# First transformer block of a three-layer f32 kernel: the projections, the long convolution, the norms and the output product in another order

## What is computed

```python
h = rms_norm(x, pre_mix_g[l])
u = h @ w_in[l]                                   # 256x1024 @ 1024x2560
u_conf, u_sc, u_att, u_lru = jnp.split(u, splits, axis=-1)
y_a = conformer_conv_mixer(...)   # val * sigmoid(gate), causal conv of 31 taps, group norm, silu
y_b = short_conv_mixer(...)       # b_gate * conv of 3 taps (c_gate * xs)
y_c = moba_attention(u_att)       # 256 rows, 4 heads of 64: here plain causal attention with ALiBi
y_d = rglru_mixer(...)            # conv of 4 taps, two gates, a linear scan over the rows, * gelu(gate)
y = jnp.concatenate([y_a, y_b, y_c, y_d], axis=-1) @ w_out[l]
x = x + rms_norm(y, post_mix_g[l])
h = rms_norm(x, pre_mlp_g[l])
m = jnp.square(jax.nn.relu(h @ mlp_w1[l])) @ mlp_w2[l]
x = x + rms_norm(m, post_mlp_g[l])
```

## Time and profile before

| | us |
|---|---|
| median of 3 runs | 1889.55 (1889.2 to 1892.25) |
| the profiled execution: time | 1888.89 |
| the profiled execution: span, first to last instruction | 1887.2 |
| the mixer's block in it | 0.3 to 158.4 |

### The profile page before, as it was taken

How to read it: one execution, slowest core, us unless ns; L and a number is a source line. 1 busy time by engine, 2 the same in 40 slices (tenths; PEclk the granted TensorE clock), 3 DMA queues, 4 the chain that set the end, 5 groups by cost and what they waited for, 6 DMA issues and landing times.

```text
span 1887.2 us, 21638 instructions
## 1 busy us (share of the span) xinstructions
PE 1387.0 (73%) x7036; PEld 562.5 (30%) x7036; DVE 1168.3 (62%) x2679; ACT 597.3 (32%) x1522; POOL 551.6 (29%) x629
## 2 busy tenths in 40 slices
PE   6978999997886555668877875497687855655665
PEld 5835566664331110123222221132232311101010
DVE  2553144125786777685688536866886478677764
ACT  2041111122433333343334323342443243332332
POOL 2002043002433333332333323322333233333432
PEclk9978999998997666779867897799888977776667
DMA  9036478634999999999999999999999999999997
GB/s 336 31 129 241 164 276 335 266 124 185 418 419 420 420 421 421 421 410 418 418 409 396 415 417 420 417 377 417 420 403 415 418 421 413 421 421 421 422 421 292
DMA packets 117966, 680.74 MB, mean 361 GB/s; under 512 B 11694, under 2 KB 13872, under 8 KB 49888
## 3 DMA queue, kind: packets, MB, share of 16 engines
q0 software_dynamic: 78336, 553.68, 71.1%
q1 hardware_dynamic: 39520, 125.71, 17.4%
HBM read 678.30 MB, written 1.05 MB: 360 GB/s over the span
## 4 chain that ended last, share of the span: by engine, by line
DMA 36%; PE 32%; DVE 11%; ACT 4%; issue 3%; DVEq 2%; POOL 2%; ACTq 1%; POOLq 0%
DMA big<-in_peer_uv,expert 33%; PE ps L584 7%; PE ps L742 6%; PE ps L1774 6%; PE ps L1785 6%; DVE big L597 5%; DMA big<-in_w_kv 2%; DVEq L463 2%; POOL big L555 2%; PE ps L328 2%; DMA normed<-in_peer_uv,expert 1%; PE ps L569 1%; ACT placed L632 1%; ACT placed L628 1%; PE ps L746 1%
## 5 line engine op out<-in xcount | busy, mean ns | idle before, releaser
L584 PE MATMUL ps<-big,placed 128*32 128x512 f32 x1992 | 597.5, 797 | 387.3 <-ACT placed L632 385.4
L597 DVE CUSTOM_DVE_ANT_0 big<-big,ps 128x1024 f32<-128x1024 f32 x498 | 595.1, 1219 | 324.1 <-DMA big<-in_peer_uv,expert 307.4
L555 POOL DMA_INDIRECT big<-in_peer_uv,expert x498 | 475.6, 955 | 1028.5 <-PE ps L584 855.1
L628 ACT ACTIVATE placed<-sel,dots 128x32 f32<-128x32 f32 x512 | 163.3, 319 | 776.5 <-DVE dots L597 769.7
L584 PEld LDWEIGHTS ps<-big,placed 128*32 128x32 f32 x1992 | 81.2, 122 | 820.1 <-ACT placed L632 740.1
L742 PE MATMUL ps<-big 128*128 128x512 f32 x384 | 191.7, 636 | 12.7 <-DVE big L1065 6.5
L632 ACT ACTIVATE placed<-placed,gate 128x32 f32<-128x32 f32 x512 | 164.6, 321 | 36.5 <-issue 1.7
L1774 PE MATMUL ps<-ua,big 128*128 128x256 f32 x512 | 116.8, 382 | 0.0
L1785 PE MATMUL ps<-big,sc 128*128 128x512 f32 x256 | 115.5, 595 | 0.0
L742 PEld LDWEIGHTS ps<-big 128*128 128x128 f32 x384 | 71.2, 200 | 129.6 <-issue 108.9
L1774 PEld LDWEIGHTS ps<-ua,big 128*128 128x128 f32 x512 | 98.1, 192 | 26.9 <-issue 15.0
(11 more groups left out here) (349 smaller groups left out, 1318.3 us busy)
## 6 DMA issues: line engine op xcount, KB each, us to landing
big<-in_mlp_w SPq DMA_DIRECT2D x16, 2048.0 KB, 10.9
big<-in_peer_wq SPq DMA_DIRECT2D x2, 8192.0 KB, 26.5
big<-in_w_kv SPq DMA_DIRECT2D x32, 512.0 KB, 15.8
big<-in_peer_wq SPq DMA_DIRECT2D x32, 512.0 KB, 14.1
big<-in_w_in SPq DMA_DIRECT2D x5, 2048.0 KB, 17.6
big<-in_peer_uv,expert POOLq DMA_INDIRECT x530, 14.9
big<-in_w_q SPq DMA_DIRECT2D x16, 512.0 KB, 10.7
big<-in_w_o SPq DMA_DIRECT2D x16, 512.0 KB, 12.8
```

The lines of the kernel that those rows point to most:

```text
L555: nc.gpsimd.indirect_dma_start(out=pair_row(n), out_offset=None, in_=rows, in_offset=bass.IndirectOffsetOnAxis(ap=expert[:, n // TOPK % DE ...
L584: last = nc.tensor.matmul(acc[r:r + TOK, :], placed[:, n % RING, :], pair_row(n)[:, D + BANK * half:D + BANK * (half + 1)], start=(opens a ...
L597: nc.vector.tensor_tensor_reduce(out=row, in0=row, in1=rows_x, scale=1.0, scalar=0.0, op0=ALU.mult, op1=ALU.add, accum_out=dots[:, u % 2, ...
L628: a.activation(to, sel32[:], ACT.Gelu, scale=dots[:, u % 2, k:k + 1])
```

## The change

It gives the mixer's block another order; the products, their shapes and what is computed stay as they are.

- x is loaded tile by tile; each tile is squared, normed and transposed by itself. The first activation is now a square root on a constant, whose table is loaded before x arrives.
- The projections run in the order 0, 1, 8, 5, 6, 7 (long convolution, LRU input, q, k, v), then 2, 3, 4, 9. The attention's scores stand before pair 2; the group mean and LRU gates before pair 3; the variance and transposes before pair 4; weights times v before pair 9. The weights' DMAs are issued in the order 0, 4, 2, 3, 1.
- The 31 taps are written out. Each instruction waits for the tap before of its own half c, which is the instruction before the last; loop and drains are gone.
- The short convolution and the end of the group norm move behind the LRU's scan or between its steps.
- The output product does tile 0 with all eight k and then tile 1. Tile 0's transposes for the MLP stand behind six of tile 1's eight k. The norms of tile 0 are all done before those of tile 1, in scratch of their own (`x1_squared`, `x1n`).

```diff
-                sp.dma_start(h[:, 0:NT, :], x[0].rearrange("(t p) d -> p t d", p=P)).then_inc(S("x_loaded"), 16)
+                w_in_v = w_in[0].rearrange("(k p) n -> p k n", p=P)
+                x_v = x[0].rearrange("(t p) d -> p t d", p=P)
+                for t in range(NT):
+                    sp.dma_start(h[:, t, :], x_v[:, t, :]).then_inc(S(f"x{t}_loaded"), 16)
...
-                w_in_v = w_in[0].rearrange("(k p) n -> p k n", p=P)
-                for c in range(5):
+                for c in (0, 4, 2, 3, 1):
...
-                act.wait_ge(S("x_loaded"), 16)
+                act.wait_ge(S("eps_ready"), 1)
+                step(act, a.activation(stats[:, 5:6], eps_col[:], ACT.Sqrt), "act_order")
                 for t in range(NT):
-                    step(act, a.activation(ua[:, 0:D], h[:, t, :], ACT.Square, accum_out=stats[:, t:t + 1]), "x_squares")
-                act.wait_ge(S("x_var"), 1)
-                step(act, a.activation(stats[:, 4:6], stats[:, 2:4], ACT.Sqrt), "x_std")
+                    act.wait_ge(S(f"x{t}_loaded"), 16)
+                    act_squares(act, P, t, "x", ua[:, 0:D])
...
-                for pair, b, to in ((2, 6, ub), (3, 7, uc), (5, 1, uq), (6, 2, uk), (7, 3, uv)):
-                    act.wait_ge(S("u_done"), pair + 1)
-                    step(act, a.activation(to, cut(bank(b), 0, NC, T), ACT.Copy), "u_out")
-                act.wait_ge(S("u_done"), 9)
                 act.wait_ge(S("constants_ready"), 5)
-                step(act, a.activation(xpad[:, :, LRU_K - 1:], cut(bank(6), 0, NC, T), ACT.Copy), "u_out")
-                act.wait_ge(S("gn_var"), 1)
-                step(act, a.activation(uc, sg, ACT.Sqrt), "gn_std")
-                act.wait_ge(S("u_done"), 10)
-                step(act, a.activation(gg, cut(bank(7), 0, NC, T), ACT.Gelu_apprx_tanh), "u_out")
+                copied(3, xpad[:, :, LRU_K - 1:], 6)
+                copied(4, uq, 7)
+                copied(5, uk, 0)
+                copied(6, uv, 1)
...
+                copied(7, ub, 0)
...
+                copied(8, uc, 0)
...
+                act.wait_ge(S("u_done"), 10)
+                step(act, a.activation(gg, cut(bank(0), 0, NC, T), ACT.Gelu_apprx_tanh), "u_out")
+                step(act, a.activation(stats[:, 5:6], eps_col[:], ACT.Sqrt), "act_order")
...
-                with dve.Fori(1, CONF_K) as tap:
+                step(dve, v.tensor_tensor(zpad[:, :, CONF_K - 1:], cut(bank(4), 0, NC, T), sg, ALU.mult), "z_ready")
+                for tap in range(CONF_K):
                     for c in range(NC):
-                        v.scalar_tensor_tensor(conv[:, c], zpad[:, c, bass.ds(tap, T)],
-                                               vec[:, bass.ds(tap * NC + (V_CONF + c), 1)], conv[:, c],
-                                               ALU.mult, ALU.add)
-                    dve.drain()
-                dve.drain().then_inc(S("conv_done"), 1)
-
-                dve.wait_ge(S("u_done"), 5)
...
+                        if tap:
+                            dve.wait_ge(S(f"conv{c}_taps"), tap)
+                            at = V_CONF + tap * NC + c
+                            last = v.scalar_tensor_tensor(conv[:, c], zpad[:, c, tap:tap + T], vec[:, at:at + 1], conv[:, c],
+                                                          ALU.mult, ALU.add)
+                        else:
+                            last = v.tensor_scalar(conv[:, c], zpad[:, c, 0:T], vec[:, V_CONF + c:V_CONF + c + 1],
+                                                   vec[:, V_DWB + c:V_DWB + c + 1], ALU.mult, ALU.add)
+                        last.then_inc(S(f"conv{c}_taps"), 1)
+
+                dve.wait_ge(S("u_out"), 2)
...
+                dve.wait_ge(S("u_done"), 9)
+                dve.wait_ge(S("u_out"), 7)
+                step(dve, v.tensor_tensor(spad[:, :, SC_K - 1:], cut(bank(6), 0, NC, T), uc, ALU.mult), "xs_used")
...
-                pe.wait_ge(S("x_normed"), NT)
                 for t in range(NT):
+                    pe.wait_ge(S("x_normed"), t + 1)
...
-                for pair, b in ((0, 4), (1, 5), (2, 6), (3, 7), (4, 0), (5, 1), (6, 2)):
+                for pair, b in ((0, 4), (1, 5), (8, 6), (5, 7), (6, 0)):
...
-                pe.wait_ge(S("u_out"), 3)
-                project(8, 6)
-                project(9, 7)
-                pe.wait_ge(S("conv_done"), 1)
-                pe.wait_ge(S("constants_ready"), 10)
-                m.matmul(bank(4), group_mean[:], conv, start=True, stop=True).then_inc(S("gn_mean"), 1)
-                pe.wait_ge(S("u_out"), 6)
-                pe.wait_ge(S("xs_used"), 1)
+
+                pe.wait_ge(S("z_ready"), 1)
+                pe.wait_ge(S("u_out"), 4)
...
+                project(2, 0)
+                for c in range(NC):
+                    pe.wait_ge(S(f"conv{c}_taps"), CONF_K)
+                pe.wait_ge(S("u_out"), 5)
+                pe.wait_ge(S("constants_ready"), 10)
+                m.matmul(bank(1), group_mean[:], conv, start=True, stop=True).then_inc(S("gn_mean"), 1)
...
+                pe.wait_ge(S("u_out"), 6)
+                project(3, 0)
+                pe.wait_ge(S("gn_sq"), 1)
+                m.matmul(bank(1), group_mean[:], sg, start=True, stop=True).then_inc(S("gn_var_done"), 1)
...
-                pe.wait_ge(S("u_out"), 7)
+                pe.wait_ge(S("lru_sigmoid"), 2 * NC)
+                project(4, 6)
...
-                pe.wait_ge(S("w_out_loaded"), 16)
-                for t, ks in ((0, (2, 3, 0, 1)), (1, (2, 3, 0, 1)), (0, (4, 5, 6, 7)), (1, (4, 5, 6, 7))):
-                    for k in ks:
-                        for first, signal in ((2, "y_b"), (0, "y_a"), (4, "y_c"), (6, "y_d")):
-                            if k == first and t == 0:
-                                pe.wait_ge(S(signal), 1)
...
+                pe.wait_ge(S("u_out"), 7)
+                project(9, 0)
+
+                def x1_transposes(t):
                     pe.wait_ge(S("x1_normed"), t + 1)
...
+                pe.wait_ge(S("w_out_loaded"), 16)
+                order = (0, 1, 4, 5, 2, 3, 6, 7)
+                for t in range(NT):
+                    for i, k in enumerate(order):
+                        if k % 2 == 0:
+                            pe.wait_ge(S(("y_a", "y_b", "y_c", "y_d")[k // 2]), 1)
+                        for half in range(2):
+                            last = m.matmul(bank(2 + 2 * t + half), yt[:, k, P * t:P * (t + 1)],
+                                            wout[:, k, BANK * half:BANK * (half + 1)], start=(i == 0), stop=(i == KD - 1))
+                        if (t, i) == (1, 5):
+                            x1_transposes(0)
+                    last.then_inc(S("y_done"), 1)
+                x1_transposes(1)
+
+        forget({"gain0_loaded", "gain1_loaded", "meta_loaded", "w1_0_loaded", "w1_1_loaded", "w2_0_loaded", "h2_t", "dve_order", "act_order"})
```

More of the change, by code:

```diff
@@ L1322, in _ @@
-                dve.drain().then_inc(S("conv_done"), 1)
-                dve.wait_ge(S("u_done"), 5)
-                dve.wait_ge(S("u_out"), 3)
-                step(dve, v.tensor_tensor(spad[:, :, SC_K - 1:], cut(bank(0), 0, NC, T), uc, ALU.mult), "xs_used")
-                for c in range(NC):
-                    chain(v.tensor_scalar(uc[:, c], spad[:, c, 0:T], vec[:, V_SC + c:V_SC + c + 1], None, ALU.mult))
-                for tap in range(1, SC_K):
-                    for c in range(NC):
-                        col = V_SC + tap * NC + c
-                        chain(v.scalar_tensor_tensor(uc[:, c], spad[:, c, tap:tap + T], vec[:, col:col + 1], uc[:, c],
-                                                     ALU.mult, ALU.add))
@@ L1335, in _ @@
-                dve.wait_ge(S("gn_mean"), 1)
-                chain(v.tensor_tensor(gd, conv, cut(bank(4), 0, NC, T), ALU.subtract))
-                step(dve, v.tensor_tensor(sg, gd, gd, ALU.mult), "gn_sq")
-                step(dve, v.tensor_tensor(yt[:, 2:4], ub, uc, ALU.mult), "y_b")
-                dve.wait_ge(S("gn_var_done"), 1)
-                step(dve, v.tensor_scalar(sg, cut(bank(5), 0, NC, T), GN_EPS, None, ALU.add), "gn_var")
-                dve.wait_ge(S("u_out"), 7)
+                step(dve, v.tensor_tensor(zpad[:, :, CONF_K - 1:], cut(bank(4), 0, NC, T), sg, ALU.mult), "z_ready")
@@ L1360, in _ @@
                                                   ALU.max, negate=True), "att_max")
-                dve.wait_ge(S("gn_std"), 1)
-                chain(v.reciprocal(sg, uc))
-                chain(v.tensor_tensor(gd, gd, sg, ALU.mult))
-                for c in range(NC):
-                    step(dve, v.tensor_scalar(gd[:, c], gd[:, c], vec[:, V_GNG + c:V_GNG + c + 1],
-                                              vec[:, V_GNB + c:V_GNB + c + 1], ALU.mult, ALU.add), "gn_out")
+                dve.wait_ge(S("gn_mean"), 1)
+                chain(v.tensor_tensor(gd, conv, cut(bank(1), 0, NC, T), ALU.subtract))
+                step(dve, v.tensor_tensor(sg, gd, gd, ALU.mult), "gn_sq")
```

(32 more changed lines are left out.)

68 lines of the change are left out of this document (32 added, 36 removed).

## The result

The changed kernel took 1869.42 us (median of 4 runs, 1867.85 to 1871.72) beside 1890.11 for the kernel before: ratio 0.9887, 95% interval 0.9874 to 0.9899, or 20.7 us less. The direction and the places were right; the gain was 4.8 us larger than the 15.9 of the forecast. Run again beside the best variant, where the kernel before took 1894.16, the ratio was 0.9891 (0.9875 to 0.9908).

The account below looks back on a forecast made before the run. The block was taken as start, projections, VectorE/ScalarE small steps, product and tail in series. Output product 19.3 earlier (start's 4.0 included), -1.8 transposes, +0.2 tail, -1.8 clock: gain 15.9, 1889.55 to 1873.6 us, range 1870 to 1881.5.

Parts of the forecast that it names:

- pairs 0 and 1: First two projection pairs on TensorE: 15.6 us as before, keeping the clock's loss of 1.8.
- the wait before pair 3: TensorE before pair 3, waiting for ScalarE to empty bank 0 behind the exponentials: 0.7 us, pair 3 starting at 71.0.
- The start: Block's beginning up to the first projection: 15.6 instead of 19.62, a gain of 4.0 us, with the first weights landing last.
- The taps: Long convolution on VectorE: written-out taps 0.40 us apart, 24.0 in place of 40.6, ending at 59.0.
- VectorE's work behind pair 3: Variance, copies, reciprocal, scan and short convolution on VectorE from 78.9 on: ends near 96, y_b asked for at 105.8.
- 12x0.23: Twelve transposes between the variance and pair 4, priced at 0.23 us each, ending at 81.7.
- 3.25: Weights times v between pairs 4 and 9, priced at its earlier duration of 3.25 us, ending at 91.9.
- half of 3.68: Tile 0's transposes for the MLP, now inside the output product: a loss of 1.8 us.
- the gates: LRU gates before pair 3: 8 records taking 1.75 us at clock 1.00 in place of 3.75 at 0.50.
- The assumed fall of the clock: Sparse stretches between the middle's dense pairs: one fall costing 1.8 us, cutting the gain from 17.7 to 15.9.
- The slower rival: Clock stays low between small products; pairs 2, 3, 4, 9 cost 6.9 us more each: 1899.5 us, chance 0.03.
- The tail: Behind the output product, 10.54 us before: loses only the wait behind tile 0's transposes, some 0.2 us.

Follow-up runs that it names:

- best: Changed kernel with matmuls of zeros in TensorE's idle time at start and tail, and tile 0's transposes behind the output product: 1869.36 us, ratio 0.9865 to the kernel before.
- taps_serial: Changed kernel with each of the 60 taps waiting for the one just before it: 1880.94 us, ratio 0.9948 to the kernel before.
- taps_only: Kernel before with the 31 taps written out and nothing else changed: 1891.61 us, ratio 1.0003 to the kernel before.
- loop_back: Changed kernel with the hardware loop for the taps put back, all else as changed: ratio 0.9989 to the kernel before.
- awake_start: Changed kernel with matmuls of zeros before x's transposes (10) and before the first pair (14): ratio 0.9881 to the kernel before.
- mid_awake: Kernel before with matmuls of zeros before the gates (16) and before the transposes of the attention's weights (30): ratio 0.9996 to the kernel before.
- transposes_behind: Changed kernel with tile 0's eight transposes behind the output product instead of inside it: ratio 0.9889 to the kernel before.

## Why the prediction was right and wrong

"Worth" is what the kernel gained (+) or lost (-) beside the prediction, in us.

| term | predicted | measured | worth |
|---|---|---|---|
| first pair | 15.6 | 15.77 | -0.2 |
| pairs 0 and 1 (to ScalarE's first step behind pair 1) | 15.6 | 32.44-15.77 = 16.7 | -1.1 |
| twelve transposes | 2.8 | 80.87-79.56 = 1.3 | +1.5 |
| weights times v | 3.25 | 89.63-87.90 = 1.7 | +1.5 |
| tile 0's transposes in the product | 1.8 | 0.9 | +0.9 |
| falls of the clock in the middle | 1.8 | none | +1.8 |
| end of the tail to the MLP | 158.46-156.48 = 2.0 | 138.19-135.72 = 2.5 | -0.5 |

They add up to 3.9 of the 4.4 by which the block's gain (158.46-138.19 = 20.3) is above the 15.9; the rest are tenths, such as the wait before pair 3 (0.3 in place of 0.7).

- **The start** was right: 4.0 predicted, 19.62-15.77 = 3.8 measured, with the weights' landing last, as said. Its clock wasn't: pairs 0 and 1 lost 2.8 in place of 1.8.
- **The taps** were right: 23.83 us for 60, end at 59.7 against 59.0. Each tap lasts 0.473 and the next starts 0.397 behind it. The rule of the Trainium skill ("VectorE: DVE Perf Modes", "The DRAIN you can't avoid") that I weighed, that the next op doesn't start until the pipe is empty, isn't what these taps show; the same section says that an op that isn't held starts earlier, which I had left out, and the 0.397 agrees with that. taps_serial, with 0.52, shows the price of waiting for the one just before.
- **That neither the taps nor the order gains by itself** the prediction didn't say; its sum implies it, and taps_only and loop_back show it.
- **VectorE's work behind pair 3** ended at 95.84 (y_b), against "near 96", and is asked for 7 us into the product; right.
- **The step that failed** is "12x0.23", "3.25" and "half of 3.68": three durations of small products at clock 0.50 put into a sum in which the clock was to be 1.00. They measured 1.3, 1.7 and 0.9, so these three terms are 3.9 us of gain that I missed. The earlier trace rows had the level, 0.50 from 100 to 118, where the first two of them stood. For the gates I had made that correction (3.75 to 1.75; measured 1.89). For the transposes I hadn't. The prediction doesn't say why: those at the start took the same 0.23 each where the windows show PEclk 1.00 (window 7 to 11 of the changed kernel above: 18 matmuls in 3.83 us). That column doesn't tell the level there: in awake_start the first zeros take 4.45/10 = 0.45 each under a PEclk of 1.00 and the sixteen transposes behind them 2.56 in place of 3.65. For weights times v I had no reason.
- **The clock isn't all of it.** The 12x0.23 was also VectorE's pace: in mid_awake, at full clock, the same twelve still took 2.7, as each head waited for VectorE. They take 1.3 in the changed kernel because the clock is up and because VectorE has scaled all heads by 74.25 (71.44+2.81), five microseconds before the first of them. So a gap that was filled changed both here. Weights times v has the clock's mark alone: most of its records last 0.27 and lasted 0.42 before.
- **The assumed fall of the clock** didn't come. I had taken the transposes' length for a sparse stretch of 3.8 us; it lasted 2.2 (78.70 to 80.87), and PEclk is 1.00 from 23 to 125. So this error comes in part from the one above. Without a fall the forecast's sum was 1889.55-17.7 = 1871.8; with the three terms as measured it is 1867.9. The losses that I had too small (start 0.2, pairs 0 and 1 1.1, the time to the MLP 0.5) bring it back to 1869.7. That the time came out only 0.6 below the range is partly luck: misses of 5.7 us one way met 1.8 the other way.
- **The slower rival** (clock low throughout) didn't happen; loop_back and taps_serial show the loss where TensorE does idle in front of a pair (4.2 and 5.9 us): 2.7 to 2.9 us more for that pair.
- **The tail**: the transposes inside the product were priced as a loss of 1.8 with 0.2 back; measured 0.9 with 0.8 back (transposes_behind). The product's new order brought nothing: from its start to the tail's last write it is 39.1 (135.72-96.66), and it was 38.4 before (156.48-118.06). Nearly all of the gain lies ahead of the output product.

## What to carry to other kernels

Here a long run on one engine and a chain on two others, one behind the other, could be laid side by side only with both halves of the change: a faster chain alone turned 17 us into a wait, and the new order alone met the old chain. When such a stretch gets dense, price its TensorE work at the clock it will have and with its operands ready, not at the clock and pace it had while it waited: here three groups of small products took 3.9 us less than in the rows of before. And an in-place update that alternates between two halves can wait for the last but one instruction instead of the last: here 24 us instead of 31.

## What I had not expected

- At the start of a trace the granted clock of the windows shows 1.00 whatever the matmuls do. In awake_start it is 1.00 over 2.5 to 7 and over 7 to 15.9, yet a 128x512 bf16 matmul takes 0.45 us from 2.54 on and 0.23 from 10.19 on (3.19 us for 14).
- With the same instructions at the same place the clock was down after the idling behind the filler matmuls in one run (best, 2.4 us of idling) and not in another (awake_start, 2.5 us). Without filler, the first five pairs took 36.3 to 37.4 us in the six traces of kernels with the new start and order, which is why their marks scatter by a microsecond.
- From the end of the last transposes to the MLP's first matmul TensorE idled 3.51 in the kernel before and in mid_awake, and 3.87 to 4.38 in the other kernels without filler there; what holds the barrier longer was not found.
